# Low parts of ten down-projection weight units formed by an accumulating DMA on GpSimd's queue

## The reference

```python
h = rms_norm(x, ln_mix_w[i])
proj = h @ w_in[i]                          # 2048 x 9216
...
x = x + merged @ w_out[i]                   # 2048 x 2048
h2 = rms_norm(x, ln_ffn_w[i])
u = causal_depthwise_conv(h2 @ w_up[i], conv_w[i], conv_b[i])
u_gate, u_val = jnp.split(u, 2, axis=-1)
x = x + (jax.nn.silu(u_gate) * u_val) @ w_down[i]      # 5504 x 2048
h3 = rms_norm(x, ln_ple_w[i])
x = x + jax.nn.sigmoid(h3 @ w_ple_gate[i]) * (p[i] @ w_ple[i])
...
```

## Time and profile before

| what | value |
|---|---|
| three executions | 1428.69, 1428.85, 1429.17 us |
| profiled execution, first to last instruction | 1427.1 us |
| median minus that span | 1.75 us |
| PE busy | 1417.3 us (99%) |
| DVE busy | 1072.4 us (75%) |
| ACT busy | 786.4 us (55%) |
| POOL busy | 152.7 us (11%) |
| mean granted TensorE clock | 0.998 of full speed |
| down projection in the trace | about 1089 to 1320 us |

### The profile page before, as it was taken

The page is one execution under the profiler, slowest core; times in us unless marked ns, Lnnn a source line. Parts: engine busy times, 40 slices in busy tenths (PEclk is TensorE's granted clock), DMA queues, the critical chain, the costliest instruction groups (busy, mean ns, idle before and its releaser), DMA issues.

```text
span 1427.1 us, 19876 instructions
## 1 busy us (share of the span) xinstructions
PE 1417.3 (99%) x7076; PEld 1204.1 (84%) x7076; DVE 1072.4 (75%) x1366; ACT 786.4 (55%) x955; POOL 152.7 (11%) x103
## 2 busy tenths in 40 slices
PE   9999999999999999999999999999999999999997
PEld 7888888888888888888888888888888888888886
DVE  7676777878687878777777777777777888888755
ACT  7555655545455555565555555555555555555544
POOL 0044144100000000000111101101011000000000
PEclk9999999999999999999999999999999999999999
DMA  9655555455755675566656666566665556565653
GB/s 324 199 175 164 155 172 171 145 188 163 232 190 179 212 247 196 168 211 182 198 170 201 183 191 194 173 199 186 191 194 179 200 198 200 170 213 199 232 200 121
DMA packets 190877, 273.48 MB, mean 192 GB/s; under 512 B 11744, under 2 KB 103136, under 8 KB 190688
## 3 DMA queue, kind: packets, MB, share of 16 engines
q1 hardware_dynamic: 190384, 272.30, 59.7%
q10 hardware_dynamic: 432, 0.37, 0.1%
HBM read 270.53 MB, written 2.10 MB: 191 GB/s over the span
## 4 chain that ended last, share of the span: by engine, by line
PE 98%; DVE 1%; issue 0%; DMA 0%; ACT 0%; SPq 0%; ACTq 0%; POOLq 0%; POOL 0%; DVEq 0%
PE aux L915 11%; PE main L915 11%; PE main L700 10%; PE main L701 10%; PE main L702 10%; PE aux L924 6%; PE main L924 6%; PE main L758 5%; PE main L760 5%; PE main L759 5%; PE aux L758 3%; PE aux L760 3%; PE aux L759 3%; PE aux L702 2%; PE aux L700 2%; PE aux L701 2%
## 5 line engine op out<-in xcount | busy, mean ns | idle before, releaser
L1523 DVE TENSOR_TENSOR w_lo<-raw,w_hi 128x1024 fp32r<-128x1024 f32 (+1 forms) x478 | 587.7, 1241 | 291.8 <-ACT w_hi L1208 291.1
L1208 ACT ACTIVATE w_hi<-raw 128x1024 fp32r<-128x1024 f32 (+1 forms) x478 | 502.1, 1052 | 469.6 <-PE main L702 133.8
L700 PE MATMUL main<-w_hi,xT 128*128 128x512 f32 x510 | 201.5, 395 | 0.4 <-DVE w_lo L2032 0.3
L701 PE MATMUL main<-w_lo,xT 128*128 128x512 f32 x510 | 198.6, 389 | 0.0
L702 PE MATMUL main<-w_hi,xT 128*128 128x512 f32 x510 | 198.6, 389 | 0.0
L915 PE MATMUL aux<-xT,w_hi 128*128 128x512 f32 x704 | 169.7, 391 | 0.0
L915 PE MATMUL main<-xT,w_hi 128*128 128x512 f32 x672 | 162.8, 391 | 0.0
L915 PEld LDWEIGHTS aux<-xT,w_hi 128*128 128x128 f32 x704 | 129.4, 188 | 25.0
L915 PEld LDWEIGHTS main<-xT,w_hi 128*128 128x128 f32 x672 | 123.2, 188 | 23.6
L2140 POOL TENSOR_TENSOR act<-cv 128x512 f32<-128x512 f32 (+1 forms) x22 | 71.9, 3267 | 418.5 <-DVE cv L1747 418.5
L700 PEld LDWEIGHTS main<-w_hi,xT 128*128 128x128 f32 x510 | 95.8, 188 | 20.2 <-DVE xT L1550 1.2
(11 more groups left out here) (334 smaller groups left out, 2180.6 us busy)
## 6 DMA issues: line engine op xcount, KB each, us to landing
raw<-in_w_up SPq DMA_DIRECT2D x336, 256.0 KB
raw<-in_w_in SPq DMA_DIRECT2D x136, 512.0 KB
raw<-in_w_down SPq DMA_DIRECT2D x84, 512.0 KB
raw<-in_w_out SPq DMA_DIRECT2D x32, 512.0 KB
raw<-in_w_ple_gate SPq DMA_DIRECT2D x32, 512.0 KB
raw<-in_w_branch_a SPq DMA_DIRECT2D x16, 512.0 KB
raw<-in_w_branch_b SPq DMA_DIRECT2D x16, 512.0 KB
raw<-in_w_in SPq DMA_DIRECT2D x15, 256.0 KB, 5.7
```

Source lines behind the costliest of these rows:

```text
L700: pe.matmul(acc, th, wh, start=first, stop=False)
L701: pe.matmul(acc, th, wl, start=False, stop=False)
L1208: ac.activation(w_hi[:, u % RING, :, 0:w], raw[:, u % RING, :, 0:w], ACT.Copy).then_inc(hi_full, 1)
L1523: dve.tensor_tensor(w_lo[:, u % RING, :, 0:w], raw[:, u % RING, :, 0:w], w_hi[:, u % RING, :, 0:w].bitcast(F32), ALU.subtract).then_inc(lo ...
```

## The change

For the ten units named above DVE's subtraction is left out. ACT writes the negated high part, `Copy` of `raw` with scale -1 into the `w_lo` slot, right behind its ordinary copy into `w_hi`, and counts `hi_negated`. POOL waits for that count and issues a DMA from `raw` to `w_lo` with `accum_op=add`, 128x1024 values (512 KB), so that `w_lo` becomes `raw - high`. The DMA counts `lo_added` of its ring slot up by 16 when it has landed. PE, and SP's load into the same slot four units later, wait for `lo_added` instead of `lo_full` for these ten units; `lo_split` corrects the count of `lo_full` for all others.

```diff
+LO_BY_DMA = [down_unit(p, i, 1) for p in range(2) for i in (6, 9, 12, 15, 18)]
+def lo_split(u):
+    return u + 1 - sum(v <= u for v in LO_BY_DMA)
...
+        hi_negated, lo_added = sem("hi_negated"), [sem(f"lo_added{r}") for r in range(RING)]
...
+        def lo_arrived(eng, u, it=None):
+            if it is None and u in LO_BY_DMA:
+                eng.wait_ge(lo_added[u % RING], 16 * sum(v <= u and v % RING == u % RING for v in LO_BY_DMA))
+            else:
+                eng.wait_ge(lo_full, plus(lo_split(u), 2 * UK, it))
...
             def slot_split(u, it=None):
                 if u >= RING:
-                    sp.wait_ge(lo_full, plus(u - RING + 1, 2 * UK, it))
+                    lo_arrived(sp, u - RING, it)
...
             def down_plain(u, p, i, a):
-                pe.wait_ge(lo_full, u + 1)
+                lo_arrived(pe, u)
...
                 ac.activation(w_hi[:, u % RING, :, 0:w], raw[:, u % RING, :, 0:w], ACT.Copy).then_inc(hi_full, 1)
+                if it is None and u in LO_BY_DMA:
+                    ac.activation(w_lo[:, u % RING, :, :], raw[:, u % RING, :, :], ACT.Copy, scale=-1.0).then_inc(hi_negated, 1)
...
             def split_lo(u, it=None):
-                if u >= UNITS:
+                if u >= UNITS or (it is None and u in LO_BY_DMA):
                     return
...
+            for k, u in enumerate(LO_BY_DMA):
+                pool.wait_ge(hi_negated, k + 1)
+                pool.dma_start(w_lo[:, u % RING, :, :], raw[:, u % RING, :, :], accum_op=ALU.add).then_inc(lo_added[u % RING], 16)
             root(2)
```

More of the change, by code:

```diff
@@ L704, in unit @@
             def unit(u, c, i, n, hi, lo, k, it=None, width=NCOL, tiles=2):
-                pe.wait_ge(lo_full, plus(u + 1, 2 * UK, it))
+                lo_arrived(pe, u, it)
                 for a in range(tiles):
@@ L1168, in _ @@
                 for j in range(SPLIT_TB):
-                    pe.wait_ge(lo_full, u + j + 1)
+                    lo_arrived(pe, u + j)
                     for a in range(2):
@@ L1175, in _ @@
                     main_released(c - 1)
-                pe.wait_ge(lo_full, u + SPLIT_TB + 1)
+                lo_arrived(pe, u + SPLIT_TB)
                 if tb == 0:
```

## The result

The changed kernel takes 1460.66 us (median of 4, 1459.82 to 1462.63), the kernel before beside it 1428.82 us: ratio 1.0225, 95% interval [1.0212, 1.0237]. It is slower, by 32 us. The profiled execution took 1459.82 us with a span of 1458.0 us, 30.9 us longer than the 1427.1 us of before.

What follows compares the result with a forecast made beforehand. PE's matmuls were taken to bound the down projection; eight stalls of 3.5 us and two of 5.1 give 38 us, 1427.1 + 38 = 1465, plus 1.75 to the median: 1467 us. Own range 1433 to 1489, with hidden case 1428 to 1494.

Steps and rivals of the forecast that it cites:

- What bounds the kernel: Down projection: PE's matmuls set its length, so taking 12.2 us off DVE can shorten it by 0.2 us at most.
- ACT's negations cost nothing: Ten added copies of 1061 ns on ACT, hidden by its idle time of 1.82 us; otherwise 1 us a unit.
- The time available: From the end of ACT's negation to PE's start of the unit: 3.84 us; a longer D stalls PE.
- 2.26 + 3.54: The DMA alone: 2.26 us fixed plus two passes of 1.77 us for two operands read, 5.8 us.
- The overlap with the loads: Delay of the DMA by SP's burst of three loads: 3.1 us in each half's first touched unit, 1.5 us afterwards.
- D: Time from the negation's end to the DMA's landing: 8.9 us in each half's first touched unit, 7.3 in the others.
- Unit 19 stands for all ten: Down projection: unit 19's timing, with ACT's copy repeating every 15.64 us, was taken for all ten units.
- two streams share the engines evenly: DMA engines: loads left beyond the DMA's fixed part delay it by as much, 3.1 or 1.5 us.
- The rhythm after a stall: SP's next burst is released about 8.0 us after PE's start, leading the negation by 3.8 us instead of 2.2.
- the rival: The clock falls to the 1.2 GHz level at each stall, 2.7 us more a unit, 1494 us; chance 0.10.
- The page that spoke for less: Skill's estimate for a GpSimd DMA: 3.2 us, or 4.4 with bytes counted twice; 0 or 6 us of stall in all.
- No cost on SP: SP's fourth load of a cycle and later ones wait for the landing; 1 us of reserve (5.03 against 4.03) covers it.

Runs made afterwards that it cites:

- scheme-unit run: The change with its ten DMAs moved to the first unit of each scheme pair (units 10, 16, ... instead of 13, 19, ...): 1431.58 us, ratio 1.0018.
- the separate run: The change without POOL's DMAs: ACT still writes ten negated copies, then DVE subtracts as in the kernel before: 1430.41 us, ratio 1.0012.
- price run: The kernel before plus nine POOL DMAs after its last store, one at a time, accumulating 512 KB and 256 KB, plain 512 KB: 1463.96 us.
- two-unit run: The change applied to units 19 and 69 only, instead of ten units: 1437.35 us, ratio 1.0058.
- run 256: Not a separate run: the words are "price run" followed by "256 KB", its three accumulating 256 KB DMAs on the kernel before, 3.2 us each alone.
- plain copies: The change with each accumulating DMA replaced by a plain copy of raw to w_lo, giving another product: 1449.23 us, ratio 1.0139.
- halves: The change with negation and DMA for only the first row tile (256 KB) of the ten units, DVE subtracting the second: 1449.79 us, ratio 1.0154.
- held-load run: The change with SP issuing the burst of loads only once the DMA has landed: 1511.65 us, ratio 1.0577.
- negate-first run: The change with ACT's negated copy placed ahead of its copy into w_hi; PE and SP's load also wait for hi_full: 1465.35 us, ratio 1.0259.

## Why the forecast held, step by step

- *What bounds the kernel.* Right. DVE gave back 10.8 us and nothing of it came off the time; the scheme-unit run has them gone too and isn't faster.
- *ACT's negations cost nothing.* Right in the change; the separate run bounds it by 1.6 us. They end where the prediction put them, 2.0 us behind the start of the ordinary copy (1116.99 to 1118.99).
- *The time available.* 3.84 us, right: the time from the end of each negation to the landing, less 3.84, gives the stall, 8.97 - 3.84 = 5.1 at the first (4.85 measured), 4.80 - 3.84 = 1.0 at the second (1.0).
- *Right mechanism, sizes off.* The stalls were to be 38 us and are 22.5. Two terms were mis-sized. The DMA's own cost "2.26 + 3.54" = 5.8 is 4.7 by the price run: with two operands, 512 KB more of the DMA cost 2.4 us against the 3.54 that two passes of a load's 1.77 made. The overlap with the loads is off too. For the eight units behind the first of each half the loads were to lead by 3.8 us and lead by 4.0 in the mean, yet D was to be 7.3 and is 5.7: 1.1 of the difference is the own cost, 0.5 the overlap, forecast as 1.5 and about 1.0. In the first unit of the second half 8.9 was forecast and 5.97 came, since the loads lead there by 3.4 us and not by 2.2: "Unit 19 stands for all ten" holds for ACT's copy, not for the loads of the second half, as the two-unit run shows. In the first unit of all 8.9 was forecast and 8.97 came by luck: the own cost is 1.1 us less, the wait for the loads as much more. 8 x 1.55 + 2.9 = 15.3 is the difference between the unrounded 37.8 and 22.5.
- *The law in its place.* I let two streams share the engines evenly. The runs at this place fit a simpler sum: the three loads and the DMA are through when all their bytes are, counted from the burst's first load, and an earlier issue of the DMA doesn't change that. By the earlier trace rows the loads alone last 7.56 us; 2 x 1.22 us for the two operands (by the price run 256 KB with two operands cost 1.2 us) make 10.0, measured 9.3 to 10.3 in nine of ten. With 1.22 us more instead of 2.44 it makes 8.8; measured 8.0 to 8.7 for most of the plain copies and 8.2 to 8.8 for most of the halves. Where the burst leads by 4.8 us, the DMA is at its floor (4.67 to 4.97). The sum was made from these runs, and it isn't a rule for other places: for the two loads ahead of each DMA in the scheme-unit run it gives 2.26 + 2 x 1.77 + 2.44 = 8.2 us, and nine of ten landings came after 9.0 to 10.5. In those nine the two loads are issued 2.3 us apart or more, wider than the 1.77 us that one takes, so bytes alone don't fill the time.
- *The rhythm after a stall.* The mechanism is right, the size a little low: the next burst is issued 8.1 to 9.5 us after a landing, 8.7 in the mean (forecast 8.0). With 9.7 us to the next landing and a cycle of 15.64 us, 8.7 + 9.7 - 15.64 = 2.8 us a cycle, of which 1.9 are the mean stall and most of the rest is matmuls at the lower clock. When the clock has fallen, PE's unit takes longer, the burst gains lead, and the next stall is short: 0.9 to 1.2 us behind the three falls with a unit after them in the same half, 1.9 to 2.9 in the five other cycles. By these rows a fall gives back some 1.5 of the 1.7 to 2.4 us that it takes, one unit later. That the mean lead came out at 4.0 us, near the 3.8 forecast, is partly due to it: 3.5 without a fall, 4.8 behind one.
- *The clock.* The forecast put no fall in its sum and gave the rival 0.10, with 2.7 us each. It came in part: four falls, 2.4 and 1.7 us each, 7.5 us in all. The objection that a stall of some 3 us ends as the clock comes down was wrong for these: in the three stalls of 2.7 to 2.9 us it came down some 0.6 us behind their end, when PE was at work again. These falls made up a half of what the stalls were short, and brought the total nearer to the forecast than its terms were: 1467 against 1460.7 us is a difference of 6 us, in part by luck, where the stalls are off by 15. Two of the prediction's own signs failed with it: PE's busy time was to be unchanged and rose by 10.3 us, and a low clock in the stage was to mean that the forecast was wrong.
- *The page that spoke for less.* The Trainium skill's "DMA: Bandwidth & Descriptors", section "Anatomy of one DMA — SWDGE (gpsimd) path", gave an estimate of 4.4 us with the bytes counted twice; the price run agrees (4.41 to 4.60), for a DMA alone. The two source reads of "Collectives: The Full Stack", section "The bandwidth ceiling: the fold count and why AG ≠ RS ≠ AR", point the same way as 4.4 against 2.9 us; whether the copy is twice as fast can't be told, since it has a price for one size alone. For the change both leave out the queue beside it, which cost more than the DMA's own excess of 0.9 us a unit.
- *No cost on SP.* Right: nothing waits for a high part or a weight sum. The held-load run shows what it costs when that reserve is overdrawn.

Left open: the clock's share is read from rows; no run has the same stalls without falls, so what the change would cost at a steady clock was not tried. Nor do the runs explain why the landings of the first and last of the ten come 0.5 to 1.5 us later after their first load than the others in most of the kernels. The first has the shortest lead, which went with late landings in the negate-first run as well; the last has not. No version found beats the kernel before, and with PE busy 99% of its span none of these could.

## What to carry to other kernels

Before work is moved to a DMA, don't size its landing by its own length but look at the loads that will be in flight: for a burst issued back to back, count from its first load and add all bytes, and take that as a lower bound where the loads come spaced out. Then ask how long before its use the operand is there: the same ten DMAs cost 32 us at one unit and 3 us at another three units earlier. And before a wait is added to a load to make room, follow that load's slot through every engine's fixed order; what stands behind it there pays.

## What was not expected of the hardware

- A POOL-issued accumulating DMA within SBUF: 4.4 us for 512 KB, 3.2 for 256 KB, a plain one of 512 KB 2.9; POOL's instruction itself takes 0.86 us accumulating and 0.54 plain.
- Issuing such a DMA up to 1 us earlier beside three 512 KB loads doesn't bring its landing forward (9.2 to 11.0 us after the first load, against 9.3 to 10.8).
- The granted clock fell to the 1.2 GHz level with each stall of 2.7 us or more (2.7, 2.8, 2.9, 4.1 and 4.9 us) and after none of 2.2 us or less in the change and the two-unit kernel, and each fall cost 1.7 to 2.7 us of matmul time. The traces of the other experiments have no exception.
